# Seven half-token products for two output tiles (Strassen's algorithm) in the MLP up projections

## What is computed

```python
def squared_relu_mlp(h, w1, w2):
    return jnp.square(jax.nn.relu(h @ w1)) @ w2
...
        h = rms_norm(x, g[2])
        x = x + rms_norm(squared_relu_mlp(h, mlp_w1[i], mlp_w2[i]), g[3])
```

## Time and profile before

| | |
|---|---|
| three runs | 1766.36, 1766.42, 1768.12 us; median 1766.42 |
| profiled execution, first to last instruction | 1764.2 us |
| median less that span (start and end around it) | 2.2 us |
| PE / PE weight load / DVE / ACT / POOL busy | 1737.4 / 1445.3 / 785.8 / 662.9 / 876.9 us |
| granted TensorE clock, mean | 0.996 |

### The profile page before, as it was taken

The page is one execution under the profiler, slowest core; times in us unless marked ns, Lnnn a source line. Parts: engine busy times, 40 slices in busy tenths (PEclk is TensorE's granted clock), DMA queues, the critical chain, the costliest instruction groups (busy, mean ns, idle before and its releaser), DMA issues.

```text
span 1764.2 us, 22985 instructions
## 1 busy us (share of the span) xinstructions
PE 1737.4 (98%) x8243; PEld 1445.3 (82%) x8243; DVE 785.8 (45%) x1225; ACT 662.9 (38%) x1039; POOL 876.9 (50%) x473
## 2 busy tenths in 40 slices
PE   8999999999999999999999999999999999999999
PEld 6887888888888877878888888889878888888887
DVE  6558654301331479956430133137856344444200
ACT  6338543312322456554321232135357332222221
POOL 3457545444444469755544444445445544444442
PEclk9999999999999999999999999999999999999999
DMA  5531123223333213123333332322210233332332
GB/s 190 133 98 59 37 72 107 95 95 96 96 96 99 80 48 108 60 84 95 103 99 96 96 95 95 95 84 72 87 49 14 95 95 96 97 101 98 96 107 71
DMA packets 46073, 158.45 MB, mean 90 GB/s; under 512 B 5744, under 2 KB 6000, under 8 KB 46000
## 3 DMA queue, kind: packets, MB, share of 16 engines
q1 hardware_dynamic: 46000, 157.45, 28.5%
HBM read 153.10 MB, written 2.10 MB: 88 GB/s over the span
## 4 chain that ended last, share of the span: by engine, by line
PE 90%; DVE 5%; ACT 2%; issue 1%; POOL 1%; DMA 0%; SPq 0%; DVEq 0%; POOLq 0%; ACTq 0%
PE PS L1834 26%; PE PS L1835 26%; PE PS L1836 26%; PE PS L1903 2%; DVE PS L1219 1%; PE PS L1939 1%; PE PS L1934 1%; PE PS L1935 1%; PE PS L2095 1%; PE PS L1844 1%; PE PS L1876 0%; PE PS L1976 0%; DVE PS L1211 0%; PE PS L2118 0%; PE PS L2119 0%
## 5 line engine op out<-in xcount | busy, mean ns | idle before, releaser
L548 POOL TENSOR_TENSOR wl<-raw,wh 128x1024 fp32r<-128x1024 f32 x216 | 523.0, 2422 | 623.2 <-ACT wh L742 198.3
L1835 PE MATMUL PS<-XLR,wh 128*128 128x512 f32 x1216 | 474.2, 390 | 0.0
L1834 PE MATMUL PS<-XHR,wh 128*128 128x512 f32 x888 | 348.8, 393 | 6.3 <-POOL wl L618 5.8
L1836 PE MATMUL PS<-XHR,wl 128*128 128x512 f32 x888 | 346.4, 390 | 0.0
L1834 PE MATMUL PS<-HH,wh 128*128 128x512 f32 x688 | 267.6, 389 | 0.0
L1835 PE MATMUL PS<-HL,wh 128*128 128x512 f32 x688 | 267.6, 389 | 0.0
L1836 PE MATMUL PS<-HH,wl 128*128 128x512 f32 x688 | 267.6, 389 | 0.0
L1835 PEld LDWEIGHTS PS<-XLR,wh 128*128 128x128 f32 x1216 | 229.1, 188 | 47.0
L728 ACT ACTIVATE wh<-raw 128x1024 fp32r<-128x1024 f32 x123 | 128.9, 1056 | 242.2 <-PE PS L1836 197.6
L1834 PEld LDWEIGHTS PS<-XHR,wh 128*128 128x128 f32 x888 | 167.4, 188 | 42.0 <-POOL wl L618 6.2
L1836 PEld LDWEIGHTS PS<-XHR,wl 128*128 128x128 f32 x888 | 167.4, 188 | 35.4
(11 more groups left out here) (344 smaller groups left out, 2561.6 us busy)
## 6 DMA issues: line engine op xcount, KB each, us to landing
raw<-weights SPq DMA_DIRECT2D x287, 512.0 KB, 3.5
X<-x_t SPq DMA_DIRECT2D x8, 256.0 KB, 6.7
out_t<-X SPq DMA_DIRECT2D x8, 256.0 KB, 4.7
KH<-rope_h SPq DMA_DIRECT2D x4, 128.0 KB, 4.7
KL<-rope_l SPq DMA_DIRECT2D x4, 128.0 KB, 5.5
QH<-XHR SPq DMA_DIRECT2D x16, 32.0 KB, 2.0
QL<-XLR SPq DMA_DIRECT2D x16, 32.0 KB, 2.0
pos_i<-positions SPq DMA_DIRECT2D x1, 256.0 KB, 8.5
```

The source lines that it names most:

```text
L548: pool.tensor_tensor(wl[:, j], raw[:, j], wh[:, j].bitcast(F32), ALU.subtract).then_inc(w_lo, 1)
L1834: pe.matmul(out, wa, xa, start=start, stop=False)
L1835: pe.matmul(out, wa, xb, start=False, stop=False)
L1836: return pe.matmul(out, wb, xa, start=False, stop=stop)
```

## The change

Four chunks of 8 up tiles and 8 down tiles of 24 matmuls take the place of two chunks of 16 and 8. Of each layer's four up chunks the first is made as before. In the other three, two output tiles (two blocks) are made together as a 2x2 product of halves: the weights' k halves by the two output tiles, the activations' k halves by 256-token halves. Winograd's form of Strassen's algorithm needs seven products of halves where the direct form has eight; a product of halves is 4 k-tiles by 3 passes, with 256 tokens. There are 4 groups a chunk, 12 a layer, 24 in all.

What is added around it:
- Activation combinations, once a layer, during the first down chunk: DVE multiplies the residual with gain and 1/rms (8 instructions of 128x2x256 into `CF`), makes four differences of 128x1024, ACT rounds 7 combinations of 128x1024 to `CH`, DVE subtracts 7 of 128x1024 to `CL`.
- Weight combinations, for each group: DVE makes four sums of 128x512 (`first_sums`, `last_sum`) in `sqb` and in place in `raw`; ACT rounds and POOL subtracts a11 (128x512), s12 (two halves, 128x1024), mid (128x1024), s4 (128x512) and a22 (128x512), in place of two whole blocks of 128x1024. Seven of eight half slots of `wh` and `wl` are used; each combination has the same slot in all groups of a chunk.
- Output sums: PE accumulates in the banks alpha, beta and gamma; ACT copies alpha and beta to quarters of `tmp` (four copies of 128x256) between products, DVE adds three of 128x256, squares two of 128x512. Both tiles of the group leave this way, without `r2`.

Other moves: `low_taps` stands in the last down chunk of layer 0; an additional block "even" (64 KB, 128x128 on ACT and POOL, no matmul) stands ahead of layer 1's MLP, so that `hi(n + 2)` of its third block is issued at the boundary and not before it; the loops over up tiles are written out; hidden tiles are consumed in the order 0, 4, 1, 5, ... .

The diff, cut to its core (the bodies of `low_*` and `high_*` each hold one wait on their source, one on the slot and one instruction):

```diff
-CHUNK = 16
+CHUNK = 8
...
+_PHASES += [("pw1", 16 + KT + 1, 16 + KT), ("pw2", 8, 8), ("even", 1, 0)]
...
+HALF_K, HALF_T = KT // 2, S // 2
+PAIRS_UP = CHUNK // 2
+ORDER = [(i % 2) * PAIRS_UP + i // 2 for i in range(CHUNK)]
+COMBO = {name: i for i, name in enumerate(["b11", "t3", "b21", "b22", "t1", "t2", "t4"])}
...
+        MH = at("MH", A, 0, [P, CHUNK, S], F32R)
+        ML = at("ML", A, 16 * KB, [P, CHUNK, S], F32R)
+        CH = at("CH", A, 32 * KB, [P, 7, HALF_K, HALF_T], F32R)
+        CL = at("CL", A, 60 * KB, [P, 7, HALF_K, HALF_T], F32R)
+        CF = at("CF", A, 60 * KB, [P, 7, HALF_K, HALF_T])
+        raw_halves = raw[:].rearrange("p r (h k) m -> p (r h) k m", h=2)
+        wh_halves = wh[:].rearrange("p r (h k) m -> p (r h) k m", h=2)
+        wl_halves = wl[:].rearrange("p r (h k) m -> p (r h) k m", h=2)
+        sums = sqb[:].rearrange("p h (k m) -> p h k m", m=P)
...
+            def load_groups(layer):
+                for c in range(1, NCHUNK):
+                    n0 = BLOCK0[f"mlp{layer}_up{c}"]
+                    for g in range(PAIRS_UP):
+                        n, q = n0 + 2 * g, up_group(layer, c, g)
+                        if g < 2:
+                            sp.wait_ge(w_lo, n - RING + 2)
+                        else:
+                            sp.wait_ge(a22_lo, q - 1)
+                        sp.dma_start(raw[:, (n + 1) % RING], weights[n + 1]).then_inc(raw_in[(n + 1) % RING], 16)
+                        if g >= 2:
+                            sp.wait_ge(w_lo, n - RING + 2)
+                        sp.dma_start(raw[:, n % RING], weights[n]).then_inc(raw_in[n % RING], 16)
+                    if c < NCHUNK - 1:
+                        load_range(n0 + CHUNK, n0 + 2 * CHUNK)
...
+            def quick_lows(layer):
+                lo_range(BLOCK0[f"mlp{layer}_up0"] + 4, BLOCK0[f"mlp{layer}_up1"])
+                for c in range(1, NCHUNK):
+                    n0, q0 = BLOCK0[f"mlp{layer}_up{c}"], up_group(layer, c, 0)
+                    low_a11(n0, n0, q0)
+                    low_s12(n0, q0)
+                    low_mid(n0, n0, q0)
+                    for g in range(PAIRS_UP):
+                        n, q = n0 + 2 * g, q0 + g
+                        low_a22(n0, n, q)
+                        if g < PAIRS_UP - 1:
+                            low_a11(n0, n + 2, q + 1)
+                        low_s4(n0, n)
+                        if g < PAIRS_UP - 1:
+                            low_s12(n0, q + 1)
+                            low_mid(n0, n + 2, q + 1)
+                    if c < NCHUNK - 1:
+                        lo_range(n0 + CHUNK, n0 + 2 * CHUNK)
...
+                if entry == "x3":
+                    hi(n + 2)
...
+            def quick_up(layer, c):
+                n0, T0 = BLOCK0[f"mlp{layer}_up{c}"], TILE0[f"mlp{layer}_up{c}"]
+                q0, h0 = up_group(layer, c, 0), (layer * NCHUNK + c) * CHUNK
+                for g in range(PAIRS_UP):
+                    n, q, more = n0 + 2 * g, q0 + g, g < PAIRS_UP - 1
+                    high_a22(n0, n)
+                    sc.wait_ge(quick, 6 * q + 1)
+                    sc.wait_ge(hid, h0 + max(2 * g - 1, 0))
+                    sc.activation(z_part(0, 0), alpha(T0, g), ACT.Copy).then_inc(z_copied, 1)
+                    if g:
+                        sc.wait_ge(bank_free, T0 + 2 * g)
+                        sc.activation(MH[:, PAIRS_UP + g - 1], tmp[:, 1], ACT.Copy).then_inc(hid_hi, 1)
+                    if more:
+                        high_a11(n0, n + 2, q + 1, False)
+                    high_s4(n0, n, q)
+                    if not more:
+                        next_high(n + 2, 6 * q + 1)
+                    sc.wait_ge(quick, 6 * q + 2)
+                    sc.wait_ge(hid, h0 + 2 * g)
+                    sc.activation(z_part(1, 1), beta(T0, g), ACT.Copy).then_inc(z_copied, 1)
+                    sc.wait_ge(quick, 6 * q + 3)
+                    sc.activation(z_part(0, 1), alpha(T0, g), ACT.Copy).then_inc(z_copied, 1)
+                    if more:
+                        high_s12(n0, n + 2, q + 1, False)
+                        high_mid(n0, n + 2, q + 1, False)
+                    else:
+                        next_high(n + 3, 6 * q + 3)
+                        next_high(n + 4, 6 * q + 5)
+                    sc.wait_ge(z_squared, q + 1)
+                    sc.activation(MH[:, g], tmp[:, 0], ACT.Copy).then_inc(hid_hi, 1)
+                    sc.wait_ge(blocks_done, n + 2)
+                    sc.activation(z_part(1, 0), alpha(T0, g), ACT.Copy).then_inc(z_copied, 1)
...
+                    if c == 0:
+                        for i in range(7):
+                            sc.wait_ge(combined, 4 * (layer + 1))
+                            sc.activation(CH[:, i], CF[:, i], ACT.Copy).then_inc(combo_hi, 1)
...
+                sig(tt(t1, t3, b11, ALU.subtract), combined, n + 1)
+                sig(tt(t2, b22, t1, ALU.subtract), combined, n + 2)
+                sig(tt(t3, b22, t3, ALU.subtract), combined, n + 3)
+                sig(tt(t4, b21, t2, ALU.subtract), combined, n + 4)
...
+            def first_sums(n, q):
+                b0, b1 = first_half(n), first_half(n) + 2
+                v.wait_ge(raw_in[(n + 1) % RING], 16 * ((n + 1) // RING + 1))
+                v.wait_ge(s12_lo, q)
+                sig(tt(sums[:, 0], raw_halves[:, b1], raw_halves[:, b1 + 1], ALU.add), w_sums, 4 * q + 1)
+                v.wait_ge(raw_in[n % RING], 16 * (n // RING + 1))
+                sig(tt(sums[:, 1], sums[:, 0], raw_halves[:, b0], ALU.subtract), w_sums, 4 * q + 2)
+                sig(tt(raw_halves[:, b1], raw_halves[:, b0], raw_halves[:, b1], ALU.subtract), w_sums, 4 * q + 3)
+            def last_sum(n, q):
+                b0 = first_half(n) + 1
+                v.wait_ge(mid_lo, q + 1)
+                sig(tt(raw_halves[:, b0], raw_halves[:, b0], sums[:, 1], ALU.subtract), w_sums, 4 * q + 4)
...
+                for g in range(PAIRS_UP):
+                    n, q = n0 + 2 * g, q0 + g
+                    if g:
+                        low_hidden(g - 1, h0 + 2 * g - 1)
+                        square_second(g - 1, q - 1)
+                    last_sum(n, q)
+                    if g:
+                        low_hidden(PAIRS_UP + g - 1, h0 + 2 * g)
+                    if g < PAIRS_UP - 1:
+                        first_sums(n + 2, q + 1)
+                    v.wait_ge(quick, 6 * q + 4)
+                    v.wait_ge(z_copied, 4 * q + 3)
+                    tt(z_part(0, 0), z_part(0, 0), gamma(g), ALU.add).then_inc(z_added, 1)
+                    v.wait_ge(quick, 6 * q + 5)
+                    tt(z_part(1, 1), z_part(1, 1), alpha(T0, g), ALU.add).then_inc(z_added, 1)
+                    v.wait_ge(quick, 6 * q + 6)
+                    sig(tt(z_part(0, 1), z_part(0, 1), beta(T0, g), ALU.add), z_added, 3 * q + 3)
+                    stt(tmp[:, 0], tmp[:, 0], 0.0, tmp[:, 0], ALU.max, ALU.mult).then_inc(z_squared, 1)
...
+                        if c == 0 and m == 0:
+                            norm_halves(layer, entry)
+                        if c == 0 and m == 1:
+                            combine_halves(layer)
+                        if c == 0 and m == 3:
+                            low_halves(layer, range(0, 4))
+                        if c == 0 and m == 4:
+                            low_halves(layer, range(4, 7))
+                        if c < NCHUNK - 1 and m == 4:
+                            first_sums(n0 + CHUNK, up_group(layer, c + 1, 0))
...
+            def half_products(out, h, combo, start):
+                i = COMBO[combo]
+                for k in range(HALF_K):
+                    pe.matmul(out, wh_halves[:, h, k], CH[:, i, k], start=start and k == 0, stop=False,
+                              skip_group_check=True)
+                    pe.matmul(out, wh_halves[:, h, k], CL[:, i, k], start=False, stop=False, skip_group_check=True)
+                    ins = pe.matmul(out, wl_halves[:, h, k], CH[:, i, k], start=False, stop=k == HALF_K - 1,
+                                    skip_group_check=True)
+                return ins
+            def quick_group(n0, T0, g, q):
+                n, a, b, c = n0 + 2 * g, alpha(T0, g), beta(T0, g), gamma(g)
+                pe.wait_ge(a11_lo, q + 1)
+                if g < 2:
+                    pe.wait_ge(bank_free, T0 - 2 + 2 * g)
+                else:
+                    pe.wait_ge(z_copied, 4 * (q - 1))
+                half_products(a, slot_half(n0, 0), "b11", True).then_inc(quick, 1)
+                pe.wait_ge(s12_lo, q + 1)
+                if g >= 2:
+                    pe.wait_ge(z_added, 3 * (q - 1))
+                half_products(b, slot_half(n0, 2), "t1", True).then_inc(quick, 1)
+                pe.wait_ge(z_copied, 4 * q + 1)
+                half_products(a, slot_half(n0, 3), "t2", False).then_inc(quick, 1)
+                pe.wait_ge(mid_lo, q + 1)
```

(8 more changed lines are left out.)

259 lines of the change are left out of this document (196 added, 63 removed).

## The result

The changed kernel takes **1823.85 us** in the median (1822.52 to 1825.14, 4 runs), the kernel before 1766.39 (1765.65 to 1768.12, 4 runs) on the same chip: a ratio of **1.0323 [1.0308, 1.0338]**. The forecast was 1745.7. The profiled execution of the change has a span of 1820.7 us against 1764.2.

A forecast was written before the change was run, and what follows sets the result against it. PE alone was taken to set the time. From a span of 1764.2 us, 20.7 us less PE work gave 1743.5, plus 2.2 around it 1745.7 us; forecast 1742 to 1748 (0.78), wider range 1740 to 1753.

The forecast's parts named there:

- Work beside PE in a group: Quick groups of 10.02 us: ACT 6.5, DVE 6.8 and POOL 8.7 us all fit, and no step makes PE wait.
- PE side, 20.7 us: Quick groups: 84 half-width matmuls take 10.02 us where 48 took 10.88, gaining 0.86 us a group, 20.7 us for 24.
- Weights bound: Rival, PE in quick groups: half-wide matmuls no closer than a 188 ns weight load, +118 us, 1884; chance 0.01.
- cheaper halves: Rival, PE in quick groups: half-wide matmuls cost nearer to columns alone, gaining up to 32.6 us, 1734; chance 0.04.
- The 2.5 ns: Skill page's extra cost per PE matmul, where the rows show 13 ns; by it the gain would be 28 us, time 1738.
- ACT 6.5 us a group: ACT in a quick group: five 128x512, four 128x256 and two 128x1024 instructions, 6.5 us beside PE's 10.02.
- POOL 8.7 us: POOL in a quick group: three 128x512 and two 128x1024 instructions, 8.7 us, up from 4.8, so 87% busy.
- Once a layer, and the down phases: First down chunk's combinations (DVE 19.1, ACT 7.4 us) cost nothing, with 4 us cover; down phases also lose nothing.
- 3.3 us of 4.8: Chunk's end: the last hidden tile takes about 3.3 us through ACT and DVE; the down tile reads it 4.8 us in.
- The windows of 0.9 us: Quick groups: three slacks of 0.9 us each, before products 3, 5 and 7 need their banks; thin, but no PE wait.
- PE waits a little: Rival, quick groups: PE waits of 0.3 to 0.7 us each give 1753 to 1762, POOL-paced 1752; chance 0.12.
- the ring: Rival, quick groups: waits circling through all engines; POOL or a landing 2.7 us late costs PE 1.5 us, 1782; chance 0.05.

The follow-up runs named there:

- a7: Changed kernel, with odd groups' product results in other SBUF buffers and ACT's copies waiting for hidden tiles two groups back: 1819.69 us, ratio 1.0283 to before.
- a2: Changed kernel, with DVE's four weight sums a group cut to one column, POOL left whole: 1809.35 us, ratio 1.0216 to before.
- a1: Changed kernel, with POOL's five subtractions a group cut to one column, so low parts of combined weights are left out: 1765.16 us, ratio 0.9987 to before.
- a6_split_lows: Changed kernel, complete, with ReLU on ACT into PSUM, squares there, and POOL's a22 and s4 subtractions moved to DVE: 1752.11 us, ratio 0.991 to before.
- a6_again: Changed kernel with ReLU on ACT, squares in PSUM and two POOL subtractions on DVE, measured once more on another chip: 1751.25 us, ratio 0.99 to before.

## Why the prediction was wrong

**What failed is the step "Work beside PE in a group": "DVE: eight of 128x512 (0.70)", and with it the overlap, "All fit".** The earlier trace rows hold 0.70 us for instructions with one input in PSUM (`HL<-PS,HH`), and the new ones have the same shape but both inputs in SBUF: four sums, two squares, two low parts. I matched rows by shape and not by where the operands lie. With POOL at 8.7 us a group there is no time in which these eight can avoid it, so the two sums that I compared with 10.02 one by one, 6.8 and 8.7, had to be added where exclusive: 13.5 us. By that sum the forecast would have been four groups less the free first one, some 3 x 3.4 = 10 us of waits a chunk, slower by a large margin; measured are 8.3. Both of the prediction's own signs of a wrong mechanism came: waits of PE released by ACT's copy, and one by POOL's `wl` at product 6.

The trace of before held the rows that would have told it, outside the MLP, in the final FFN stage, where POOL works beside DVE (source view of the kernel before, min/median/max ns):

```profile
L1211 DVE TENSOR_TENSOR tmp<-tmp,sqb x22: 694/2466/2466, 1424.8 to 1643.0; 128x512 f32<-128x512 f32 x22
...
L1211 DVE TENSOR_TENSOR HL<-tmp,HH x22: 691/693/2672, 1428.6 to 1646.2; 128x512 f32 x22
```

A median of 2.47 us for a 128x512 product in SBUF, 0.69 at the least, and 2.67 at most for exactly the low part that the quick products make: the same line, L1211, that gives 0.69 in the rows that I read. The spread between minimum and maximum was the sign.

The same stage holds a limit of theory A as I put it. A DVE copy with a single input in SBUF also stood still beside POOL (source view, then the timelines of DVE and POOL):

```profile
L1820 DVE CAST HH<-tmp x22: 426/427/2482, 1426.0 to 1645.6; 128x512 f32 x22
```

```profile
1426.02 2.48 DVE L1820 CAST HH<-tmp 128x512 f32 x1 [0.15 <-DVE tmp L1211]
```

```profile
1425.82 2.40 POOL L548 TENSOR_TENSOR wl<-raw,wh 128x1024 fp32r<-128x1024 f32 x1 [0.51 <-ACT wh L728]
```

It takes 0.43 us by itself and ends 0.28 us after POOL here. So two SBUF inputs are not the only form that waits, which the exception in the passage quoted above leaves room for. The change has no DVE copy from SBUF in its groups, and no run varied this one.

Point by point:
- *PE side, 20.7 us.* Right in kind: 84 matmuls at 0.120 give 19.2 us, the 264-wide figure as it stands. Weights bound and cheaper halves did not occur. The 2.5 ns that the prediction took from the Trainium skill ("TensorE: Matmul & The Clock Gate", Back-to-back issue gap) is given there for an isolated matmul, and the section says itself that it does not describe a stream of loads and matmuls; so 28 us and 1738 were no forecast of that page for this kernel. Nor is its Part 3 (Packing small matmuls) as strict as the prediction has it: it also lets a load into the background weight buffer go ahead of running matmuls.
- *The clock.* The prediction read the slices of the earlier trace rows as full level throughout. A digit 9 does not say that: from 599 to 847 us, between the MLPs, the kernel before has a granted clock of 0.97. Both MLPs were at 1.00, so nothing in the sum hangs on it.
- *ACT 6.5 us a group.* Right: 6.42 busy in a group of 13.44. It waits; it is not late by its own work, though PE's waits name it.
- *POOL 8.7 us.* Right in work (a first-group whole block still takes 2.40); its records hold the waiting too, so the later group shows 10.64.
- *Once a layer, and the down phases.* "3.3 us of 4.8" at each chunk's end failed by the same price: the last square and low part meet POOL's three blocks and become 2.85 and 2.12 us long, so the low part ends about 3 us late. The entry wait is 2.98 us x 6. The changed entry of layer 1 and the combinations brought no new wait of PE, though two of the combinations' 128x1024 subtractions on DVE, between 330 and 600 us, took 2.86 us each where the prediction had 1.225.
- *The windows of 0.9 us.* Their structure was right: the first group, which starts with nothing behind it, keeps them all, and the waits of later groups begin at the three places that it had called thin (products 3, 5 and 7); from the third group on product 6 waits too.
- *The rival "PE waits a little".* It took POOL's 2.85 us for a busy DVE's worst and priced POOL alone, at most 10.3 us a group. It saw that DVE stretches POOL and did not ask what POOL does to DVE.
- *The rival "the ring".* Nearest, at a chance of 0.05 and 1782: its releaser, ACT's copies in order, is what the trace names. Its price, 1.5 us a group, was too small (the later groups lose 2.4 to 3.4), and its cause (a late landing or POOL) was not this one: a7 shows the ring is only the path on which the exclusive work reaches PE.

Two things remain open. Of the six entry waits of equal length two were followed by a stretch at PE's lower clock level and four were not; in a2 it was four of six, in a1, with waits of 1.9 us, three. And the few us at the start, where the granted clock of the first 40 us was 0.91 in this profile and 1.00 in those of before and of a1. These are not the change's: a6_split_lows and a6_again are one kernel, with 1.00 and 0.91 there, and their first quick chunks begin at 338.6 and 341.3 us. What decides it no run shows.

## What to carry to other kernels

Price a VectorE instruction by where its operands lie, not only by shape: with two inputs in SBUF add its time to POOL's and hold the sum against the period, as a least time (a2 took more); a `tensor_tensor` with one input in PSUM ran free in every row here, while a copy from SBUF did not. Read minimum, median and maximum of such rows across the whole trace before trusting a mean. When the wait names a copy, ask what the chain before it does: a second buffer moved the waits here, and moving one operand into PSUM together with a fair share of POOL's work turned +3.2% into -1%.
